# Query weights of two expert heads placed and used ahead of the gathers, and one third of a head norm done in tokens by heads

## The chip, the cores and the metric

The kernel runs on one core of one Trainium2 chip. The metric is the device time of one execution in microseconds (us). All times stated as moments (645.05, say) are counted from the start of the span of the one profiled execution.

## The reference

Two transformer blocks are computed one after the other on 256 tokens of width 1024, in fp32. What matters here is the end of the second block:

```python
mixed = jnp.concatenate([sb_o, hg_o, mem_o], axis=-1)   # sb_o: 8 heads of 64, each rms-normed over its 64
x = x + mixed @ w_out[l]
x = x + peer_ffn(rms_norm_2(x, norm_ffn_gain[l]), peer_w_query[l], peer_sub_keys[l], peer_u[l], peer_v[l])

# peer_ffn, for a block of 128 tokens: 8 heads, 128 + 128 keys, top 16, 16384 experts of width 1024
q = (x_blk @ w_query).reshape(b, t, PEER_HEADS, 2, HALF_KEY)
scores = jnp.einsum('bthcd,hcnd->bthcn', q, sub_keys)
top_s, top_i = lax.top_k(scores, 16)                     # in each half
best_s, pos = lax.top_k(cand_s, 16)                      # of the 16 x 16 sums of the two halves
expert_idx = jnp.take_along_axis(cand_i, pos, axis=-1)
gate = jax.nn.softmax(best_s, axis=-1)
act = gelu(jnp.einsum('btd,bthkd->bthk', x_blk, expert_u[expert_idx]))
out = jnp.einsum('bthk,bthkd->btd', gate * act, expert_v[expert_idx])
```

## The kernel before

The kernel is written engine by engine; each engine has its own stream of instructions, carried out in order, and semaphores tie them. Work is laid out by hand.

**Dense products.** Every weight tile (1 MB, 128 partitions by 2048) is split by ScalarE (`high_parts`, L1608) into a rounded high part `d_hi` in four quarters of 512 columns, and GpSimd (L2095, quarters 0 to 2) or VectorE (L2175, quarter 3) makes the low part `v_lo`. TensorE adds three products for each (L766). The cast of a quarter waits until TensorE has used the same quarter of the tile before (`s_dused`). The last such matrix is `out2`, in two halves of the columns, n = 0 and n = 1, each summing over eight k of 128 features. Its features are `hT_hi` and `hT_lo`: k = 0, 1 from memory attention, and then three groups of 512 numbers for each of 128 partitions (two k each): group 0 the HGRN heads, groups 1 and 2 the stick-breaking heads.

**The norm of a group** before `out2`. ScalarE squares the PSUM result (`square`, L1919); TensorE sums over the 64 features of each head with a block matrix and gets the sum for each feature and token, 128x512 (`head_sums`, L730); ScalarE takes the root of all 128x512 (`head_roots`, L1924); VectorE the reciprocal of all 128x512 (L2788) and multiplies (L2791, `mixed_normed`); ScalarE makes the high part (`mixed_high`, L1931), VectorE the low part (`mixed_low`, L2803). VectorE's order is: norm of group 0, norm of group 1, low part of 0, norm of group 2, low parts of 1 and 2. ScalarE's order is: high part 1, the four casts of the second half of `out2` n = 0, high part 2.

**The expert phase.** There are 16 units (8 heads by 2 blocks of 128 tokens) of 16 picks each, 256 picks in all. For each pick GpSimd issues one gather (`gather`, L2085) that fetches for every token the row of its expert, u and v together, 8 KB, into one of 15 row places (`row_slots`); VectorE takes the dot of u and the normed token (`expert_dots`, L2917); ScalarE applies gelu to four picks at a time (L2014) and puts the four weights on diagonals (L2022); TensorE adds diagonal times v into PSUM (`expert_values`, L1515). That frees the place, and the gather 15 picks later may be issued (`s_vused`). The places 9 and 10 are ring slots, 11 is the room of `d_hi`, 12 that of `v_lo` (`ada`), 13 is `memT` (free since the second memory projection), and 14 is `mix_rows`, the room of `hT_hi`, which `out2` reads to its end.

**The queries.** Each head needs 1 MB of query weights. SyncE loads them through two ring slots (L700): heads 0 and 1 as `out2` frees the slots, head h from 2 on when head h - 2 has been used (`s_wqu`). TensorE computes head 0 (`first_queries`, L1424) and head 1 (`queries`, L1450; `key_scores`, L730) before the picks begin, and head 2 in four parts between the picks of unit 0, head 3 in unit 2, and so on. ScalarE copies the result out (`queries_out`, L2001). VectorE finds the best keys (`best_keys`, L2848 to L2852), the best pairs and the expert numbers of unit u + 2 while it works on unit u.

ScalarE's order at the start of the expert phase is what the change touches most:

```python
row_to_bank(0)          # L2008
queries_out(1)          # L2001
gate_exp(0)             # L1993, softmax exponentials of units 0 and 1
gate_exp(1)
for u in range(UNITS):  # gelu, diagonals, ...
```

VectorE has `gates_of(0)` and `gates_of(1)` (L2899, L2900), which wait for these exponentials, directly before the first `expert_dots`. GpSimd waits once for the end of `out2`, then for the expert numbers of each unit, and issues the gathers in order.

Of the kernel before, what the change touches and what calls it, by code (L numbers as in the profile page):

```python
# [17 lines left out]
ALU = mybir.AluOpType  # L18
ACT = mybir.ActivationFunctionType
# [116 lines left out]
EARLY_TILE = [N_TILES + 1 + PEER_HEADS + j for j in range(len(EARLY))]  # L136
QUERY_SLOT = [(N_TILES + h % 2) % RING for h in range(PEER_HEADS)]


# [13 lines left out]
def psum_plan():  # L153
# [79 lines left out]
    for n in range(2):  # L233
        for tb in range(TB):
            group(("out2", n, tb), OUT2_BANK[n, tb])
    for name, bank in UNIT0_GROUPS:
        group(name, bank)
    for h in range(1, PEER_HEADS):
        group(("wq", h), 2 + h % 2)
        group(("keys", h), 2 + h % 2)  # L240
# [61 lines left out]
def build(nc, x_in, mem_in, pos_in, vec_in, ident_in, const_in, gain_in, w_in, uv_in, out):  # L302
    with ExitStack() as ctx:
# [31 lines left out]
        def take(*shape, at=None):  # L335
# [10 lines left out]
            if len(shape) == 3:  # L346
# [124 lines left out]
                      mix_rows.rearrange("p a n -> p (a n)")]  # L471

        def expert_rows(s):

            return row_slots[s % ROWS]
# [22 lines left out]
        halfms = stat[:, 164:166]  # L498
        sel = stat[:, 166:167]
        KINDS = {"cmp": 0, "slc": 16, "win": 32, "dsa": 0, "mem": 16}  # L500

# [62 lines left out]
        s_mprob = sem("mem_probs")  # L564
        s_sq = sem("mixed_squares")
        s_on = sem("mixed_normed")
        s_zln = sem("z_log")
# [5 lines left out]
        s_keys = sem("keys_loaded")  # L573
        s_wq = [sem(f"query_weights{i}_loaded") for i in range(2)]
        s_wqu = sem("query_weights_used")
        s_rows = sem("rows_gained")
# [85 lines left out]
        def _(sp):  # L662
# [31 lines left out]
            sp.dma_start(keep, w_in[KEYS_TILE]).then_inc(s_keys, 16)  # L694
            for h in range(PEER_HEADS):
                if h < 2:
                    sp.wait_ge(s_dused, 4 * (len(DENSE) - RING + h) + 4)
                else:
                    sp.wait_ge(s_wqu, h - 1)
                sp.dma_start(ring[:, QUERY_SLOT[h], :], w_in[QUERY_TILE[h]]).then_inc(s_wq[h % 2], 16)  # L700

# [8 lines left out]
        def _(pe):  # L710
# [58 lines left out]

            def project_rows(what, group, n, width=512):  # L770

                out_ = [begin((group, n, tb) if group in ("in", "out", "out2") else (group, tb))
                        for tb in range(TB)]
                for half in range(2):
                    d = DENSE_AT[(what, n, half)]
                    for r in range(4):
# [10 lines left out]
                        if k == KD - 1:  # L787
                            last = pe.drain()
                        last.then_inc(s_dused, 1)

            def project_features(what, n, groups):
# [569 lines left out]
            def head_sums(i):  # L1361
# [3 lines left out]
                end(mm(ps[:, :], con("pairblk"), sq[:, i, :]), ("ssq", i))  # L1365

            mem_values()
            stick_sums(0)
# [18 lines left out]
            stick_values(7)  # L1387
            head_sums(2)
            project_rows("out2", "out2", 0)
            acc = {(tb, c): banks[4 + 2 * tb + c] for tb in range(TB) for c in range(2)}  # L1390
# [49 lines left out]
            def queries(h, part):  # L1440

                name = ("wq", h)
                w = ring[:, QUERY_SLOT[h], :].rearrange("p (k n) -> p k n", k=KD)
                if part == 0:
                    begin(name)
                    pe.wait_ge(s_wq[h % 2], 16 * (h // 2 + 1))
                ps = banks[PLAN[name][0]]
                for k in (2 * part, 2 * part + 1):
                    for c in range(2):
                        last = nc.tensor.matmul(ps[:, c * T:(c + 1) * T], w[:, k, c * P:(c + 1) * P], hT[:, k, :],  # L1450
                                                start=(k == 0 and c == 0), stop=(k == KD - 1), skip_group_check=True)
                if part == 3:
                    end(last, name)
                    pe.drain().then_inc(s_wqu, 1)

            def key_scores(h):

                ps = begin(("keys", h))
                for tb in range(TB):
# [46 lines left out]
            for part in range(4):  # L1506
                queries(1, part)
            key_scores(1)

            def expert_values(s):  # L1510
# [10 lines left out]
            for u in range(UNITS):  # L1521
                if u % 2 == 1 and u // 2 + 2 < PEER_HEADS:
                    key_scores(u // 2 + 2)
                for s in range(u * TOPK, (u + 1) * TOPK):
                    if s % PART == 0 and u % 2 == 0 and u // 2 + 2 < PEER_HEADS:
                        queries(u // 2 + 2, s % TOPK // PART)
                    expert_values(s)
# [3 lines left out]
        def _(act):  # L1531
# [419 lines left out]
            nc.scalar.activation(stat[:, 152:153], one, ACT.Sqrt)  # L1951
            head_roots(2)
            mixed_high(1)
# [76 lines left out]
            row_to_bank(0)  # L2030
            queries_out(1)
            gate_exp(0)
            gate_exp(1)
            for u in range(UNITS):
                for part in range(TOPK // PART):
# [7 lines left out]
                    if g == PICKS // PART - 2:  # L2043
                        result(0, 0)
                        result(0, 1)
                if u % 2 == 0 and u // 2 + 2 < PEER_HEADS:
                    queries_out(u // 2 + 2)
# [4 lines left out]
        def _(pool):  # L2052
# [26 lines left out]
            def gather(s):  # L2079
# [3 lines left out]
                if s >= ROWS:  # L2083
                    pool.wait_ge(s_vused, s - ROWS + 1)
                nc.gpsimd.indirect_dma_start(  # L2085
                    expert_rows(s), None, uv_in,
# [16 lines left out]
        def _(dve):  # L2103
# [704 lines left out]
            mixed_normed(0, ("hgo",))  # L2808
            mixed_normed(1, ("sbo", 0))
            mixed_low(0)  # L2810
            mixed_normed(2, ("sbo", 1))
            mixed_low(1)
# [239 lines left out]
```

## Time and profile before

| | us |
|---|---|
| median of 3 runs | 1329.34 (1328.43 to 1330.27) |
| the profiled execution, its own time | 1326.55 |
| its span, first to last instruction | 1324.8 |
| TensorE busy | 1151.2 (87% of the span) |
| VectorE busy | 855.0 (65%) |
| GpSimd busy | 554.7 (42%) |
| ScalarE busy | 480.8 (36%) |
| mean granted TensorE clock | 0.937 of full speed |
| bytes moved by DMA | 381.17 MB, mean 288 GB/s |
| of the chain that ended last: TensorE 42%, DMA 36%, VectorE 13% | |

The span has two halves that look quite different: up to about 645 us dense products and attention, and from there the expert phase. Busy shares over the whole span mix the two, so the table alone doesn't tell what an edit in either is worth. The "idle" figure in brackets behind a row of the timeline is the time that the engine had no work just before it, with what ended the wait.

### The profile page before, as it was taken

To read this page: it belongs to the slowest core of one execution; us is meant where nothing else is said; L and a number is where in the kernel's file an instruction comes from. 1 tells how busy PE (TensorE), PEld (TensorE's weight loads), DVE (VectorE), ACT (ScalarE), POOL (GpSimd) and SP (SyncE) were. 2 spreads that over 40 slices of the span, in tenths; PEclk is the share of its full clock that TensorE was granted. 3 is DMA by queue.
4 is the path that set the end of the run, shared out by engine and by line. 5 is a ranking of instruction groups with operands and counts; after the bars stand their busy time and mean duration, and the time that the engine had idled before them with its cause. 6 is when DMAs were issued, how large, how long until landed. Compare 5 with 4: busy or idle time off the path is not lost.

```text
span 1324.8 us, 14114 instructions
## 1 busy us (share of the span) xinstructions
PE 1151.2 (87%) x4900; PEld 749.5 (57%) x4900; DVE 855.0 (65%) x1807; ACT 480.8 (36%) x1051; POOL 554.7 (42%) x479
## 2 busy tenths in 40 slices
PE   6889899899999989999788878888788878877877
PEld 3667777699978689876643333433334334333332
DVE  5777566545463388666776767767677776677553
ACT  3363133555544566655321222212222222222111
POOL 1457332476686555413433333333333433423330
PEclk8899787999999999999988999988989999979998
DMA  9533332645476443222599999999999999999993
GB/s 382 210 142 127 128 128 76 242 160 182 169 268 222 175 161 128 95 81 95 205 421 422 421 422 421 422 422 420 421 422 420 422 421 422 421 421 421 422 421 128
DMA packets 53463, 381.17 MB, mean 288 GB/s; under 512 B 6160, under 2 KB 6544, under 8 KB 7568
## 3 DMA queue, kind: packets, MB, share of 16 engines
q0 software_dynamic: 36864, 268.45, 48.7%
q1 hardware_dynamic: 15664, 111.00, 22.6%
q8 instruction: 39, 0.64, 0.2%
q10 hardware_dynamic: 864, 0.82, 0.2%
q14 instruction: 32, 0.26, 0.1%
HBM read 379.20 MB, written 1.05 MB: 287 GB/s over the span
## 4 chain that ended last, share of the span: by engine, by line
PE 42%; DMA 36%; DVE 13%; ACT 4%; issue 3%; POOL 1%; PEldq 1%; PEld 0%; SPq 0%; DVEq 0%; POOLq 0%; ACTq 0%
DMA arena<-uv_dram,arena 25%; PE bank L766 15%; PE bank L1515 8%; PE bank L730 7%; PE row_bank L766 6%; DMA mix_rows<-uv_dram,arena 6%; PE row_bank L730 2%; DMA ada<-uv_dram,arena 2%; DVE gain_rows_in L2917 2%; DMA ring<-uv_dram,arena 2%; DMA memT<-uv_dram,arena 2%; DVE arena L2313 1%; PE bank L853 1%; DVE arena L2788 1%; POOL v_lo L2095 1%
## 5 line engine op out<-in xcount | busy, mean ns | idle before, releaser
L1515 PE MATMUL bank<-arena 128*128 128x512 f32 x684 | 337.7, 645 | 86.9 <-ACT arena L2022 86.5
L2095 POOL TENSOR_TENSOR v_lo<-ring,d_hi 128x512 fp32r<-128x512 f32 x189 | 268.8, 1436 | 286.8 <-ACT d_hi L1608 218.7
L1515 PEld LDWEIGHTS bank<-arena 128*128 128x128 f32 x684 | 137.3, 206 | 270.7 <-issue 160.8
L2085 POOL DMA_INDIRECT arena<-uv_dram,arena x171 | 163.1, 954 | 290.6 <-PE bank L1515 265.7
L1608 ACT CAST d_hi<-ring 128x512 fp32r<-128x512 f32 x200 | 120.9, 620 | 137.0 <-PE bank L766 82.1
L2917 DVE SCALAR_TENSOR_TENSOR gain_rows_in<-arena,row_bank 128x1024 f32<-128x1024 f32 x86 | 104.9, 1220 | 81.2 <-DMA arena<-uv_dram,arena 81.1
L2014 ACT ACTIVATE arena<-arena 128x4 f32<-128x4 f32 x64 | 13.1, 205 | 388.0 <-DVE gain_rows_in L2917 388.0
L2175 DVE TENSOR_TENSOR v_lo<-ring,d_hi 128x512 fp32r<-128x512 f32 x63 | 59.5, 944 | 125.3 <-ACT d_hi L1608 118.2
L2917 DVE SCALAR_TENSOR_TENSOR arena<-arena,row_bank 128x1024 f32<-128x1024 f32 x85 | 103.6, 1219 | 48.9 <-DMA arena<-uv_dram,arena 48.2
L2022 ACT ACTIVATE arena<-ident,arena 128x128 f32<-128x128 f32 x256 | 81.7, 390 | 108.6 <-DVE arena L2924 108.6
L1515 PE MATMUL bank<-ring,arena 128*128 128x512 f32 x136 | 67.0, 634 | 11.5 <-ACT arena L2022 11.3
L730 PE MATMUL bank<-arena 128*128 128x128 f32 (+5 forms) x456 | 69.4, 302 | 3.4 <-issue 1.3
L730 PEld LDWEIGHTS bank<-arena 128*128 128x128 f32 (+1 forms) x456 | 58.2, 198 | 13.4 <-issue 8.6
L766 PE MATMUL bank<-hT_hi,d_hi 128*128 128x256 f32 x208 | 59.5, 286 | 2.1 <-DVE arena L2620 1.1
L766 PE MATMUL bank<-hT_lo,d_hi 128*128 128x256 f32 x208 | 58.8, 283 | 0.0
L766 PE MATMUL bank<-hT_hi,v_lo 128*128 128x256 f32 x208 | 58.8, 283 | 0.0
L766 PE MATMUL row_bank<-hT_hi,d_hi 128*128 128x256 f32 x192 | 54.9, 286 | 3.2 <-DVE hT_lo L2162 2.4
L766 PE MATMUL bank<-d_hi,hT_hi 128*128 128x512 f32 (+1 forms) x128 | 49.9, 390 | 5.2 <-POOL v_lo L2095 2.0
L766 PE MATMUL row_bank<-hT_lo,d_hi 128*128 128x256 f32 x192 | 54.3, 283 | 0.0
L766 PE MATMUL row_bank<-hT_hi,v_lo 128*128 128x256 f32 x192 | 54.3, 283 | 0.0
L1515 PEld LDWEIGHTS bank<-ring,arena 128*128 128x128 f32 x136 | 26.9, 201 | 47.2 <-issue 32.5
L1450 PE MATMUL bank<-hT,ring 128*128 128x256 f32 x224 | 52.4, 379 | 0.0
(404 smaller groups left out, 2304.4 us busy)
## 6 DMA issues: line engine op xcount, KB each, us to landing
ring<-w_dram SPq DMA_DIRECT2D x93, 1024.0 KB, 4.8
arena<-w_dram SPq DMA_DIRECT2D x9, 1024.0 KB, 10.5
arena<-uv_dram,arena POOLq DMA_INDIRECT x171, 24.2
x<-x_dram SPq DMA_DIRECT2D x1, 1024.0 KB, 6.0
arena<-mem_dram SPq DMA_DIRECT2D x1, 1024.0 KB, 16.6
out_dram<-x SPq DMA_DIRECT2D x2, 512.0 KB, 4.9
arena<-const_dram SPq DMA_DIRECT2D x1, 868.0 KB, 17.1
ring<-uv_dram,arena POOLq DMA_INDIRECT x34, 24.8
```

Of the source, the lines that this page charges most:

```text
L730: return nc.tensor.matmul(out_, lhsT, rhs, start=start, stop=stop)
L766: last = nc.tensor.matmul(out_, l, m, start=start and part == 0, stop=stop and part == 2, skip_group_check=True)
L853: last = nc.tensor.matmul(ps[g * HD:(g + 1) * HD, :], vcol("c", 4 * half + kk).to_broadcast([P, HD]), w[:, kk, :], start=(half == 0 and kk ...
L1450: last = nc.tensor.matmul(ps[:, c * T:(c + 1) * T], w[:, k, c * P:(c + 1) * P], hT[:, k, :], start=(k == 0 and c == 0), stop=(k == KD - 1) ...
L1515: last = nc.tensor.matmul(acc[tb, c][:, :], diag[:, s % N_DIAG, :], expert_rows(s)[:, D + c * 512:D + (c + 1) * 512], start=False, stop=(s ...
L1608: nc.scalar.copy(d_hi[:, r, :], dense_quarter(d, r)).then_inc(s_dhi, 1)
L2022: nc.scalar.activation(diag[:, s % N_DIAG, :], ident[:, :], ACT.Copy, scale=coefs[:, s:s + 1]).then_inc(s_diag, 1)
L2085: nc.gpsimd.indirect_dma_start(expert_rows(s), None, uv_in, bass.IndirectOffsetOnAxis(ap=ids[:, s:s + 1], axis=0)).then_inc(s_got[s % ROWS ...
L2095: nc.gpsimd.tensor_tensor(v_lo[:, r, :], dense_quarter(d, r), d_hi[:, r, :], ALU.subtract).then_inc(s_dpl, 1)
L2175: tt(v_lo[:, 3, :], dense_quarter(d, 3), d_hi[:, 3, :], ALU.subtract).then_inc(s_dvl, 1)
L2313: ins = stt(arow[:, n, :], w[:, kk, :], vcol("c", k), arow[:, n, :], ALU.mult, ALU.add)
L2917: stt(dotted[s % 2], expert_rows(s)[:, 0:D], 1.0, row_bank[:, :], ALU.mult, ALU.mult, accum_out=dots[:, s:s + 1]).then_inc(s_dot, 1)
```

## The change

Three things are done.

1. The 1 MB query weights of heads 2 and 3 no longer go through the ring but into row places 13 (`memT`) and 14 (`mix_rows`). Head 2's load is issued right behind the keys, head 3's once `out2` is complete. Heads 4 to 7 go through the ring, heads 4 and 5 released by the use of heads 0 and 1.
2. TensorE computes the queries of heads 2 and 3 directly after the key scores of head 1, ahead of the first expert values; none are computed in units 0 and 2 any more. Both use PSUM bank 2, so head 3 waits until ScalarE has copied head 2 out. ScalarE copies both out before `gate_exp(0)`. The gather into place 13 waits for the use of head 2's weights, that into place 14 for head 3's.
3. Group 2 of the head norm is done in tokens by heads: TensorE sums with the squares as the stationary operand and two columns of the block matrix as the moving one (four products, an 128x8 result); the root and the reciprocal are taken of 128x8; eight products (a column of the reciprocals spread over 64 columns, times the identity) bring them back to features by tokens in bank 0. They stand between k = 1 and k = 2 of `out2` n = 0. VectorE copies the values out of PSUM, then multiplies. The sums wait, as before, for the squares.

```diff
+EARLY_HEADS = {2: 13, 3: 14}
...
-            for h in range(PEER_HEADS):
-                if h < 2:
+            for h in (2, 0, 1, 3, 4, 5, 6, 7):
+                if h == 2:
+                    sp.wait_ge(w_used, N_WHOLE)
+                elif h < 2:
                     sp.wait_ge(s_dused, 4 * (len(DENSE) - RING + h) + 4)
+                elif h == 3:
+                    sp.wait_ge(s_dused, 4 * len(DENSE))
                 else:
-                    sp.wait_ge(s_wqu, h - 1)
-                sp.dma_start(ring[:, QUERY_SLOT[h], :], w_in[QUERY_TILE[h]]).then_inc(s_wq[h % 2], 16)
+                    sp.wait_ge(s_wqu, h - 3 if h < 6 else h - 1)
+                sp.dma_start(query_weights(h), w_in[QUERY_TILE[h]]).then_inc(
+                    s_wqe[h - 2] if h in EARLY_HEADS else s_wq[h % 2], 16)
...
+            def last_head_sums():
+                pe.wait_ge(s_sq, 3)
+                ps = begin(("ssq", 2))
+                for kk in range(2):
+                    for tb in range(TB):
+                        at = 2 * (2 * kk + tb)
+                        last = mm(ps[:, at:at + 2], sq[:, 2, kk * T + tb * P:kk * T + (tb + 1) * P],
+                                  con("pairblk")[:, 0:P:HD])
+                end(last, ("ssq", 2))
+            def last_head_rows():
+                pe.wait_ge(s_rec8, 1)
+                ps = begin(("roots",))
+                for kk in range(2):
+                    for tb in range(TB):
+                        for j in range(2):
+                            at = 2 * (2 * kk + tb) + j
+                            last = mm(ps[j * HD:(j + 1) * HD, kk * T + tb * P:kk * T + (tb + 1) * P],
+                                      root8[:, at:at + 1].to_broadcast([P, HD]), ident[:, :])
+                end(last, ("roots",))
...
-            head_sums(2)
-            project_rows("out2", "out2", 0)
+            last_head_sums()
+            project_rows("out2", "out2", 0, behind_pair=last_head_rows)
...
             key_scores(1)
+            for h in EARLY_HEADS:
+                for part in range(4):
+                    queries(h, part)
...
-                    if s % PART == 0 and u % 2 == 0 and u // 2 + 2 < PEER_HEADS:
+                    if s % PART == 0 and u % 2 == 0 and 4 <= u // 2 + 2 < PEER_HEADS:
                         queries(u // 2 + 2, s % TOPK // PART)
...
-            head_roots(2)
+            ps = wait_full(act, ("ssq", 2))
+            ins = nc.scalar.activation(root8, ps[:, 0:8], ACT.Sqrt, bias=eps, scale=1.0 / HD)
+            free(ins, ("ssq", 2))
+            wait_read(act, ("ssq", 2))
+            nc.scalar.copy(stat[:, 153:154], one).then_inc(s_root8, 1)
...
             queries_out(1)
+            queries_out(2)
+            wait_full(act, ("keys", 1))
+            queries_out(3)
             gate_exp(0)
...
+                elif s in EARLY_HEADS.values():
+                    pool.wait_ge(s_wqu, s - EARLY_HEADS[2] + 3)
...
             mixed_normed(1, ("sbo", 0))
+            dve.wait_ge(s_root8, 1)
+            nc.vector.reciprocal(root8, root8).then_inc(s_rec8, 1)
             mixed_low(0)
-            mixed_normed(2, ("sbo", 1))
+            ps = wait_full(dve, ("sbo", 1))
+            free(nc.vector.tensor_copy(root2[:, 2, :], ps[:, :]), ("sbo", 1))
+            wait_read(dve, ("sbo", 1))
+            ps = wait_full(dve, ("roots",))
+            free(tt(sq[:, 2, :], ps[:, :], root2[:, 2, :], ALU.mult), ("roots",))
+            wait_read(dve, ("roots",))
+            nc.vector.memset(coef[:, 0:1], 0.0).then_inc(s_on, 1)
             mixed_low(1)
```

## Rows read from the trace of the kernel before

**Rows 1.** The page, parts 2 and 3: DMA share by slice; the gather queue

```profile
DMA  9533332645476443222599999999999999999993
...
q0 software_dynamic: 36864, 268.45, 48.7%
```

**Rows 2.** Busy time by windows; columns: PE, PEld, DVE, ACT, POOL, PEclk, DMA share, GB/s

```profile
705.00:730.00 25.00, 17.26 (x37) 7.17 (x35) 19.65 (x54) 4.95 (x14) 8.35 (x9) 0.86 1.01 422
...
1280.00:1305.00 25.00, 20.46 (x43) 8.32 (x42) 12.98 (x24) 5.40 (x17) 2.02 (x3) 0.93 0.81 338
```

**Rows 3.** Waits of SyncE's DMA queue: total, times, longest us

```profile
SPq L700 <- PEq L1454: 300.7, 5, 83.7
...
SPq L700 <- PEq L1503: 24.6, 1, 24.6
```

**Rows 4.** DMA issues from 643 to 650: times, KB each, median us to landing

```profile
ring<-w_dram SPq DMA_DIRECT2D x1, 1024.0 KB, 5.0
```

**Rows 5.** Timeline of GpSimd: start us, us, what, [idle before, releaser]

```profile
645.05 1.49 POOL L2085 DMA_INDIRECT arena<-uv_dram,arena  x1 [19.08 <-DVE arena L2893]
...
664.27 0.93 POOL L2085 DMA_INDIRECT mix_rows<-uv_dram,arena  x1 [0.31 <-issue]
672.42 0.94 POOL L2085 DMA_INDIRECT arena<-uv_dram,arena  x1 [7.21 <-PE bank L1515]
675.80 0.94 POOL L2085 DMA_INDIRECT arena<-uv_dram,arena  x1 [2.45 <-PE bank L1515]
```

**Rows 6.** Timeline of TensorE, 640 to 672

```profile
646.99 7.07 PE L1450 MATMUL bank<-hT,ring 128*128 128x256 f32 x32
...
655.73 1.89 PE L1450 MATMUL bank<-hT,ring 128*128 128x256 f32 x8
668.36 4.64 PE L1515 MATMUL bank<-arena 128*128 128x512 f32 x5 [10.74 <-ACT arena L2022]
```

**Rows 7.** Timeline of ScalarE, 628 to 672

```profile
654.10 0.59 ACT L2001 COPY arena<-bank 128x512 f32<-128x512 f32 x1 [7.53 <-PE bank L1450]
654.70 1.28 ACT L1993 ACT_TABLE_LOAD   x1
```

**Rows 8.** Timeline of VectorE, 628 to 700

```profile
658.30 1.22 DVE L2917 SCALAR_TENSOR_TENSOR arena<-arena,row_bank 128x1024 f32<-128x1024 f32 x1
...
663.13 1.22 DVE L2917 SCALAR_TENSOR_TENSOR gain_rows_in<-arena,row_bank 128x1024 f32<-128x1024 f32 x1 [1.31 <-DMA arena<-uv_dram,arena]
...
667.71 0.16 DVE L2924 TENSOR_TENSOR arena<-arena 128x4 f32<-128x4 f32 x1
...
692.95 1.22 DVE L2917 SCALAR_TENSOR_TENSOR gain_rows_in<-arena,row_bank 128x1024 f32<-128x1024 f32 x1 [1.26 <-DMA arena<-uv_dram,arena]
...
695.78 1.22 DVE L2917 SCALAR_TENSOR_TENSOR arena<-arena,row_bank 128x1024 f32<-128x1024 f32 x1 [1.05 <-DMA arena<-uv_dram,arena]
```

**Rows 9.** Busy time by windows, columns as in rows 2

```profile
665.00:670.00 5.00, 1.64 (x2) 0.84 (x3) 4.76 (x16) 1.28 (x4) 0.21 (x1) 0.50 1.02 428
```

**Rows 10.** DMA issues from 644.8 to 646.5: the first gather alone

```profile
arena<-uv_dram,arena POOLq DMA_INDIRECT x1, 8.1
```

**Rows 11.** Timeline of all engines around the norm of group 2

```profile
605.02 1.12 PE L730 MATMUL bank<-arena 128*128 128x512 f32 x2 [0.69 <-ACT arena L1919]
...
608.20 3.35 DVE L2788 RECIPROCAL arena<-arena 128x512 f32<-128x512 f32 x1
...
611.64 0.62 ACT L1608 CAST d_hi<-ring 128x512 fp32r<-128x512 f32 x1 [0.73 <-PE bank L766]
...
612.43 0.91 ACT L1931 ACTIVATE hT_hi<-arena 128x256 fp32r<-128x256 f32 x2 [0.18 <-DVE stat L2796]
...
613.62 0.47 PE L766 MATMUL bank<-d_hi,hT_hi 128*128 128x512 f32 x1 [2.02 <-DVE hT_lo L2803]
```

**Rows 12.** Products with few columns, TensorE's timeline at 46 us

```profile
46.41 0.95 PE L730 MATMUL bank<-stat,arena 128*128 128x1 f32 x8
```

**Rows 13.** Groups by line and shape, 0 to 600: products of 64 by 128

```profile
L730 PE MATMUL bank<-ident,arena 128*64 128x128 f32 x48 | 4.4, 355 | 3.1 <-DVE arena L2456 3.1
```

More of the change, by code:

```diff
@@ L235, in psum_plan @@
             group(("out2", n, tb), OUT2_BANK[n, tb])
+        if n == 0:
+            group(("roots",), 0)
     for name, bank in UNIT0_GROUPS:
         group(name, bank)
-    for h in range(1, PEER_HEADS):
+    group(("wq", 1), 3)
+    group(("keys", 1), 3)
+    group(("wq", 2), 2)
+    group(("wq", 3), 2)
+    group(("keys", 2), 2)
+    group(("keys", 3), 3)
+    for h in range(4, PEER_HEADS):
         group(("wq", h), 2 + h % 2)
@@ L471, in build, with query_weights @@
                       mix_rows.rearrange("p a n -> p (a n)")]
+        def query_weights(h):
+            return row_slots[EARLY_HEADS[h]] if h in EARLY_HEADS else ring[:, QUERY_SLOT[h], :]
         def expert_rows(s):
@@ L499, in build @@
         sel = stat[:, 166:167]
+        root8 = stat[:, 168:176]
         KINDS = {"cmp": 0, "slc": 16, "win": 32, "dsa": 0, "mem": 16}
@@ L565, in build @@
         s_sq = sem("mixed_squares")
+        s_root8 = sem("last_head_roots")
+        s_rec8 = sem("last_head_reciprocals")
         s_on = sem("mixed_normed")
@@ L574, in build @@
         s_wq = [sem(f"query_weights{i}_loaded") for i in range(2)]
+        s_wqe = [sem(f"early_query_weights{i}_loaded") for i in range(2)]
         s_wqu = sem("query_weights_used")
@@ L768, in three_parts, with project_rows @@
                 return last
-            def project_rows(what, group, n, width=512):
+            def project_rows(what, group, n, width=512, behind_pair=None):
                 out_ = [begin((group, n, tb) if group in ("in", "out", "out2") else (group, tb))
@@ L789, in project_rows @@
                         last.then_inc(s_dused, 1)
+                        if k == 1 and behind_pair is not None:
+                            behind_pair()
             def project_features(what, n, groups):
@@ L1442, in queries @@
                 name = ("wq", h)
-                w = ring[:, QUERY_SLOT[h], :].rearrange("p (k n) -> p k n", k=KD)
+                w = query_weights(h).rearrange("p (k n) -> p k n", k=KD)
                 if part == 0:
                     begin(name)
-                    pe.wait_ge(s_wq[h % 2], 16 * (h // 2 + 1))
+                    if h in EARLY_HEADS:
+                        pe.wait_ge(s_wqe[h - 2], 16)
+                    else:
+                        pe.wait_ge(s_wq[h % 2], 16 * (h // 2 if h > 1 else 1))
                 ps = banks[PLAN[name][0]]
@@ L1456, in key_scores @@
             def key_scores(h):
+                wait_read(pe, ("wq", h))
                 ps = begin(("keys", h))
@@ L2045, in _ @@
                         result(0, 1)
-                if u % 2 == 0 and u // 2 + 2 < PEER_HEADS:
+                if u % 2 == 0 and 4 <= u // 2 + 2 < PEER_HEADS:
                     queries_out(u // 2 + 2)
```

## The prediction
> **What bounds the kernel now.** I began with the busy tenths of the page. The DMA line jumps to 9 at slice 20 and stays there to the end [rows 1]; that is where the gathers begin. The windows make it sharp: from 680 us on every window of 25 us has a DMA share of 1.01 at 420 to 423 GB/s, and only the window from 1280 falls off, when the last gathers drain [rows 2]. In the same window TensorE is busy 17.26 and VectorE 19.65 of 25 us. So the second half is bound by the DMA engines: 256 gathers carry 268.45 MB [rows 1], 1.049 MB each, which at 422 GB/s is 2.49 us. Whatever bytes leave this phase shorten it; whatever leaves the engines empty lengthens it.
>
> VectorE's timeline says the same from the other side: it waits for a landing again and again, at 663.13, 692.95, 695.78 [rows 8], and landings come 2.5 us apart.
>
> The waits of SyncE's queue show which other bytes share this phase. One load (head 2's) was released by the end of the first queries, and five (heads 3 to 7) by the end of `queries` [rows 3]. The first gather is issued at 645.05 [rows 5]; head 2's load falls in the same 7 us, landing after 5.0 us [rows 4]. So six loads of 1 MB compete with the gathers.
>
> The first half is bound by TensorE and by hand-overs between engines; the part that the change touches ends at 645, where the first expert numbers release the gathers.
>
> **The change part by part: the loads.** Heads 2 and 3 are loaded before 645. Head 2's goes out behind the keys, about 603; head 3's when `out2` is done, about 637, and 5.0 us [rows 4] end it at 642, before the gathers. Neither delays a load that someone waits for. SyncE's queue is in order, so I looked at what stands behind head 3's load: heads 4 and 5, released at the moments at which heads 2 and 3 were released before. In the gather phase four loads are left instead of six: 2 x 2.49 = **-4.98 us**. This rests on a saturated phase, which [rows 2] shows to the end.
>
> **The queries ahead of the picks, and the new wait.** TensorE is idle for 10.74 us before the first expert value at 668.36 [rows 6]. The queries of heads 2 and 3 go into that hole, but they are longer than it, and the cost lies on ScalarE: both copies now stand ahead of the gate exponentials. What is queued behind is everything: VectorE's gates wait for them, and its first dot stands behind the gates. By the rows: head 2 starts at 655.73, and a head takes 7.07 [rows 6], so 662.8; the copy takes 0.59 [rows 7] and frees the bank, 663.5 with the hand-over; head 3 to 670.6; copy, 671.3; table load 1.28 [rows 7], 672.6; two exponentials and the second gate, about 1.7 (estimate: VectorE's first dot was at 658.30, 2.3 us behind that table load's end [rows 7, 8], part of it other work). The first dot comes at 674.3 instead of 658.30, 16.0 later.
>
> What follows runs without waits for rows, as the first four have long landed: four dots of 1.22 are 4.9, then `best_keys`, which took from 664.3 to 667.71 [rows 8], 3.4; so the first weights are formed at 682.6 and not 667.71, 14.9 later. TensorE's first value follows 0.65 later [rows 6, 8], at 683.3. Its clock was at 0.50 after the idle time [rows 9], and it will again have been idle, 12 us, so I keep the pace of before: the place of row 0 was free 4.06 after the first value, that of row 1 3.38 after that [rows 5, 6]. The 16th gather (row 15) is then issued at 687.3, not 672.42, and row 16's at 690.7, not 675.80.
>
> Does the DMA run empty? Before, rows 15 and 16 landed at 692.95 and 695.78 [rows 8]; the queue held so much that both landings came 20 us behind their issue. Now what counts is how soon a gather into an empty queue lands. No row shows one. The nearest: the first gather, 8.1 us [rows 10], which shared the engines with head 2's load (2.5 us of it at most), and a load of the same bytes by SyncE, 5.0 [rows 4]. I take 8.1 - 2.5 = 5.6, and 5.8 with a little for sharing with the row before it. Row 15 lands at max(692.95, 687.3 + 5.8 = 693.1), row 16 at 690.7 + 5.8 = 696.5 against 695.78: **+0.7 us**. With 5.0 it is nil, with 8.1 it is 698.8, +3.0. From row 17 on the pace of the places (1.72 us a row at full clock, and no query part between) beats that of the DMA (2.49), so nothing is added.
>
> VectorE makes up what it lost: a group of four picks costs it 4 x 1.22 + 3.4 = 8.3 us at most, while the DMA takes 9.96 for four rows. In a window of 25 us it had 5.35 to spare [rows 2], so 16 us are regained in some 75 us, and before that the lead of 15 places covers it.
>
> The gathers into places 13 and 14 wait for heads 2 and 3: 663.2 and 671.0. The last of them was issued at 664.27 [rows 5]. GpSimd is in order, but behind it stands only row 15's gather, which is held until 687.3 anyway, and row 14's turn at the DMA comes at about 687. Cost nil; it would cost only if head 3 ended after about 683.
>
> **The norm of group 2.** Before, TensorE stands idle 2.02 us ahead of k = 4 at 613.62, released by VectorE's low part, which came behind the reciprocal of 128x512 at 608.20, 3.35 us [rows 11]. The new path takes the 3.35 away but puts work on TensorE in front of k = 2. The sums: four products are eight records, and eight records with one column took 0.95 [rows 12], against 0.57 to the next product for the old sums (605.02 to 605.59): +0.4. The rows: eight products, 16 records; records of 64 by 128 took 4.4 / 48 = 0.092 each [rows 13], those of [rows 12] 0.119: 1.5 to 1.9, I take 1.8, nearer to the second as the operands change with each. So k = 2 and 3 come 2.2 later, and k = 3 ends when k = 4 began before, 2.02 us after its old end, to 0.2. By then VectorE has the low part of group 1: the rows are there at 611.1, the product takes 0.7, and the low part 0.9, 612.9. What is late next is ScalarE's order: the casts of quarters 2 and 3 wait for k = 2 and k = 3 (the second was at 611.64 [rows 11], now 613.9), and high part 2 stands behind them, 614.6 instead of 612.43, 0.91 long; low part 2 then ends at 616.5, and k = 6 is due at 616.4. So it just fits. **+0.1 us**, from -1.0 (if the new products cost TensorE half as much, so that half of the idle time goes) to +1.5 (if the casts or the low part come late for k = 6).
>
> **The sum** is -4.98 + 0.7 + 0.1 = -4.2 us. The profiled execution took 1326.55 (span 1324.8), which is 2.8 under the median of 1329.34; the same difference on each gives 1322.4 for an execution like the profiled one and 1325.1 for the median. Bounds: -4.98 + 0 - 1.0 = -6.0 and -4.98 + 3.0 + 1.5 = -0.5, 1323.3 to 1328.8. A difference of 0.2% (2.7 us) is about what a measurement of this kernel can tell from none.
>
> **The rivals.** (A) *No gap at all.* If a gather into a nearly empty queue lands as fast as SyncE's load (5.0), or if the queue still holds a little at 691, the restart costs nothing: -4.9, 1324.4. For it: a landing is that of the slowest of 16 DMA engines, so that engine may still have work when the others are empty, and part of any gap is hidden. The Trainium skill's page "DMA: Bandwidth & Descriptors", section "Anatomy of one DMA", gives a fit of about 2.0 us plus the bytes over 436 GB/s for a GpSimd transfer, 4.4 us here by estimate; by it row 16 would be in time and this rival would hold. No row shows an unshared gather, and 8.1 speaks against it.
>
> (B) *The gap is long.* The first gather's 8.1 holds for every restart, and the ends of the norm's bounds come with it: -4.98 + 3.0 + 1.5 = -0.5, 1328.8, no difference that can be measured. For it: GpSimd's own description of the gather and the way to the engines is in the 8.1 and isn't shared.
>
> (C) *Slower: TensorE doesn't get its clock back.* Between row 15 and the point where the places have a lead again the DMA lives on TensorE's pace. At the clock of [rows 9] a row costs 3.38 us [rows 5], 0.89 more than the DMA needs. Before, it was back at 1.0 by 675. If it stayed low for n rows from 683, the DMA would lose 0.2 + 0.89 n; the gain is used up at n = 6, and it is slower by over 0.2% from n = 9. For n = 12: +10.9 - 4.9 = +6.0, 1335.3. Against it: nothing in the picks differs from before, where the clock rose in 4 us.
>
> (D) *The change of the loads does not count*, because the places and not the bytes set the pace. Then nothing is gained and the 16 us lateness is felt in part: about 1330, no measurable difference to slightly slower. Against it stands the share of 1.01 in all windows.
>
> **How the numbers follow.** Forecast 0.57, A 0.15, B 0.16, C 0.06, D 0.06. The forecast lies under 1326.7 (faster by over 0.2%) in four fifths of its cases: 0.47, and with A 0.62. The rest of it, B and half of D give 0.28 for within 0.2%; C and half of D, with some for what I don't see, 0.10 for slower. Predicted is 1325.1. Range 1322.8 to 1329.0: it takes in the bounds and B, and leaves out C, D and the far edge of A.
>
> **What would show it.** In the profile after: SyncE's waits for `queries` fall from five to three inside the phase, or the loads there from six to four; VectorE's first dot at about 674; row 15's gather at 687 and row 16's at 691, with a short dip of the DMA share in the window 685 to 695 and 1.01 behind it; the last landing about 4 us earlier than 1310; the first gather still at 645.2. The idle time of 2.02 before k = 4 is gone and 16 new records stand in its place. The prediction is wrong if the DMA share dips for over 3 us, if the first gather moves by over 1 us, or if the DMA rate changes.

## The result and the profile after

| | before | after |
|---|---|---|
| first comparison, 6 runs each, median us | 1328.51 (1326.45 to 1330.27) | 1320.70 (1317.95 to 1324.19) |
| ratio, 95% interval | | 0.9945 (0.9927 to 0.9963) |
| two further comparisons, ratio | | 0.9955 (0.9939 to 0.9970), 0.9960 (0.9945 to 0.9975) |
| all runs of this study | 119 runs, median 1326.7, mean 1326.9 | 27 runs, median 1321.5, mean 1321.1 |
| profiled execution, own time (span) | 1326.55 (1324.8) | 1321.45 (1319.7) |

The change gains 5.8 us, plus or minus 0.9 (95%, difference of the means over all runs), where 4.2 was predicted; the measured median lies below the range. A single execution scatters by 4 us to either side, so the two medians of the first comparison, 7.8 apart, say less than all runs together.

Now the profile after. At the start of the expert phase, first TensorE, then ScalarE, then VectorE, then GpSimd (start, us, what, idle before and its releaser):

```profile
655.88 7.07 PE L1500 MATMUL bank<-hT,memT 128*128 128x256 f32 x32
663.62 7.17 PE L1500 MATMUL bank<-hT,mix_rows 128*128 128x256 f32 x32 [0.68 <-ACT arena L2059]
682.90 17.80 PE L1569 MATMUL bank<-arena 128*128 128x512 f32 x36 [12.10 <-ACT arena L2080]
...
670.89 0.58 ACT L2059 COPY arena<-bank 128x512 f32<-128x512 f32 x1 [7.32 <-PE bank L1500]
```

```profile
673.31 0.16 DVE L2970 RECIPROCAL arena<-arena 128x1 f32<-128x1 f32 x1 [16.06 <-ACT arena L2051]
...
674.25 1.22 DVE L2988 SCALAR_TENSOR_TENSOR arena<-arena,row_bank 128x1024 f32<-128x1024 f32 x1
```

```profile
645.13 1.49 POOL L2148 DMA_INDIRECT arena<-uv_dram,arena  x1 [19.05 <-DVE arena L2964]
...
671.12 0.93 POOL L2148 DMA_INDIRECT mix_rows<-uv_dram,arena  x1 [6.92 <-PEq L1504]
686.95 0.93 POOL L2148 DMA_INDIRECT arena<-uv_dram,arena  x1 [14.90 <-PE bank L1569]
689.46 0.93 POOL L2148 DMA_INDIRECT arena<-uv_dram,arena  x1 [1.57 <-PE bank L1569]
```

SyncE's waits, to be set against [rows 3]: the end of `queries` now releases three loads and not five, so four loads are left in the phase, where there were six.

```profile
SPq L721 <- PEq L1504: 296.1, 3, 204.0
```

The timelines answer to [rows 5 to 8]. VectorE's 16.06 us of idle time behind ScalarE's exponentials is the new wait: it stands still until ScalarE has copied out head 3. Its first dot moves from 658.30 to 674.25, row 15's gather from 672.42 to 686.95. The windows show what the DMA engines make of it (columns as in [rows 2]):

```profile
680.00:685.00 5.00, 2.10 (x3) 1.07 (x4) 4.79 (x17) 1.28 (x4) 0.00 (x0) 0.50 1.01 421
685.00:690.00 5.00, 5.00 (x10) 2.11 (x10) 4.79 (x15) 0.20 (x1) 1.47 (x2) 0.79 0.95 349
690.00:695.00 5.00, 5.00 (x13) 2.13 (x12) 5.00 (x11) 1.46 (x5) 3.15 (x4) 1.00 0.99 401
```

They run short by 72 GB/s for 5 us and by 20 for the next 5, together 0.46 MB or 1.1 us of their time, and are full again from 695. The last landing releases VectorE's last dot at 1304.89, where it was 1309.98 before:

```profile
1309.98 1.22 DVE L2917 SCALAR_TENSOR_TENSOR gain_rows_in<-arena,row_bank 128x1024 f32<-128x1024 f32 x1 [2.33 <-DMA arena<-uv_dram,arena]
```

```profile
1304.89 1.22 DVE L2988 SCALAR_TENSOR_TENSOR gain_rows_in<-arena,row_bank 128x1024 f32<-128x1024 f32 x1 [2.33 <-DMA arena<-uv_dram,arena]
```

And the norm, TensorE's timeline, to be set against [rows 11]:

```profile
605.75 1.05 PE L752 MATMUL bank<-arena 128*128 128x2 f32 x8 [0.69 <-ACT arena L1973]
...
609.58 1.09 PE L752 MATMUL row_bank<-ident,stat 128*64 128x128 f32 x16
610.61 0.50 PE L788 MATMUL bank<-d_hi,hT_hi 128*128 128x512 f32 x1
```

The 16 records of the new rows hold up k = 2 by 1.03 us (609.58 to 610.61), and no idle time is left ahead of k = 4.

### The profile page after: what moved, and what is told of

Read it like the earlier page. It is cut to its first block, busy times and chain, and to the rows that moved or that the text cites. A ratio compares the mean times of both kernels' runs of the same rounds, so it can differ in the third digit from the quotient of the medians.

```text
span 1319.7 us, 14169 instructions
## 1 busy us (share of the span) xinstructions
PE 1146.9 (87%) x4922; PEld 750.1 (57%) x4922; DVE 848.9 (64%) x1808; ACT 480.6 (36%) x1052; POOL 556.9 (42%) x479
## 3 DMA queue, kind: packets, MB, share of 16 engines
HBM read 379.20 MB, written 1.05 MB: 288 GB/s over the span
## 4 chain that ended last, share of the span: by engine, by line
PE 49%; DMA 31%; DVE 11%; ACT 4%; issue 3%; POOL 1%; PEldq 1%; PEld 0%; SPq 0%; DVEq 0%; POOLq 0%; ACTq 0%
DMA arena<-uv_dram,arena 22%; PE bank L788 16%; PE bank L1569 11%; PE bank L752 7%; PE row_bank L788 7%; DMA mix_rows<-uv_dram,arena 4%; PE row_bank L752 2%; DMA ada<-uv_dram,arena 2%; DMA memT<-uv_dram,arena 2%; PE bank L1500 2%; DMA ring<-uv_dram,arena 2%; DVE gain_rows_in L2988 2%; DVE arena L2376 1%; PE bank L877 1%; PE bank L1255 1%
## 5 line engine op out<-in xcount | busy, mean ns | idle before, releaser
L1569 PE MATMUL bank<-arena 128*128 128x512 f32 x684 | 333.5, 639 | 83.1 <-ACT arena L2080 82.6
L2072 ACT ACTIVATE arena<-arena 128x4 f32<-128x4 f32 x64 | 13.1, 205 | 369.7 <-DVE gain_rows_in L2988 369.7
L1569 PE MATMUL bank<-ring,arena 128*128 128x512 f32 x136 | 63.6, 608 | 11.6 <-ACT arena L2080 11.6
L752 PE MATMUL bank<-arena 128*128 128x128 f32 (+6 forms) x462 | 69.3, 300 | 3.6 <-issue 1.4
L788 PE MATMUL bank<-d_hi,up_hi 128*128 128x512 f32 x128 | 51.2, 400 | 0.6 <-issue 0.5
```

Of the source, the lines that this page charges most:

```text
L752: return nc.tensor.matmul(out_, lhsT, rhs, start=start, stop=stop)
L788: last = nc.tensor.matmul(out_, l, m, start=start and part == 0, stop=stop and part == 2, skip_group_check=True)
L1569: last = nc.tensor.matmul(acc[tb, c][:, :], diag[:, s % N_DIAG, :], expert_rows(s)[:, D + c * 512:D + (c + 1) * 512], start=False, stop=(s ...
```

## The experiments

Every profiled execution was cut at three marks: the start of the sums of group 2 on TensorE (605.02 before), the first gather (645.05) and the start of VectorE's last dot, which waits for the last landing (1309.98). The first piece is the same code in all kernels. What is left behind the last dot is 14.4 to 15.0 us in fourteen of the seventeen profiles; it is 13.1 in the third of before, and 15.9 and 13.0 in the two with the hole filled. No part of the change goes with these three, and the table leaves this last piece out.

| kernel | start of the sums | sums to first gather | first gather to last dot | both, mean | difference to before by these | measured, mean of all runs |
|---|---|---|---|---|---|---|
| before, three profiles | 605.02, 607.19, 607.46 | 40.03, 41.66, 41.62 | 664.93, 664.17, 664.16 | 705.5 | | |
| after, three profiles | 605.75, 603.80, 606.30 | 39.38, 39.35, 39.37 | 659.76, 660.34, 659.49 | 699.2 | -6.3 | -5.8 ± 0.9 |
| loads only, two | 604.65, 608.80 | 41.61, 41.60 | 660.06, 660.58 | 701.9 | -3.6 | -2.7 ± 1.0 |
| norm only, two | 603.78, 603.01 | 39.40, 39.34 | 664.31, 664.08 | 703.6 | -1.9 | -1.0 ± 1.0 |
| hole filled, two | 601.72, 602.74 | 40.02, 40.00 | 664.27, 664.22 | 704.3 | -1.2 | -2.0 ± 1.4 |
| loads, hole filled | 604.79 | 40.03 | 660.06 | 700.1 | -5.4 | -6.5 ± 1.2 |
| two loads fewer | 601.36 | 41.66 | 660.87 | 702.5 | -3.0 | -2.7 ± 1.4 |
| gates ahead, two | 602.00, 604.28 | 39.37, 39.36 | 659.16, 659.62 | 698.8 | -6.7 | -7.3 ± 1.2 |
| waits added | 603.87 | 39.36 | 659.99 | 699.4 | -6.1 | -7.0 ± 1.7 |

The last column sets the mean of each kernel's runs (6 to 27) against the mean of 119 runs of before, with 95%. All rows agree with the sum of the two pieces within it.

**The kernel before, again.**

> The kernel before, unchanged, for a second profile and more times. If the profiled execution of before (1326.55) only happened to lie low, a second profiled one will lie near 1328.5, and its trace will show where the 2 us between executions sit: in the dense half (before the first gather), or in how far the last landing stands behind the mean of the 16 DMA engines. If the two halves are fixed and the profile was typical, the second lies within 0.5 us of the first.

Measured: median 1327.18 (12 runs), ratio to before 1.0004 (0.9991 to 1.0017); its profiled execution took 1329.59, span 1327.8. So 1326.55 was not low: over 119 runs the median is 1326.7. What was high was the median of three, 1329.34. The 3 us between the two profiles sit ahead of the first gather: 2.17 before the sums, 1.63 between the sums and the gather, and -0.76 behind it. The second of these is the interesting one. TensorE's timeline behind the idle 2.02 us, and its granted clock, in this execution and (last fence) in the first:

```profile
615.79 0.47 PE L766 MATMUL bank<-d_hi,hT_hi 128*128 128x512 f32 x1 [2.02 <-DVE hT_lo L2803]
...
617.18 0.63 PE L766 MATMUL bank<-d_hi,hT_lo 128*128 128x512 f32 x1
617.60 0.63 PE L766 MATMUL bank<-d_hi,hT_hi 128*128 128x512 f32 x1
```

```profile
617.00:620.00 3.00, 3.00 (x8) 2.32 (x8) 0.04 (x1) 0.62 (x1) 1.27 (x1) 0.50 0.28 115
```

```profile
617.00:620.00 3.00, 2.74 (x13) 1.99 (x12) 0.00 (x0) 1.48 (x3) 2.89 (x3) 1.00 0.00 0
```

About 1 us after the engine has resumed, the granted clock is at 0.50 (1.2 of 2.4 GHz), and some eight products start 0.43 us apart instead of 0.23. That is the 1.63. In the first profile the same idle time has no such effect. I had only the first when I predicted.

**The kernel after, again, twice.**

> The kernel after, unchanged. Theory 1 (the change is worth what the two traces show, 5.1 us, and the 7.8 between the medians holds some chance): over more runs the difference comes down to 5 to 6.5 us. Theory 2 (the traces miss something that most executions have): it stays at 7 to 8 us, and a second profile shows the last landing 6 us or more ahead of before's.

> The kernel after, for comparison on one chip. 660 us from the first gather to the last landing, 39.4 from the sums to the first gather, and 6 us less than before on the median (4.4 from the gather phase, 1.9 on average from the norm).

Measured: medians 1321.47 (9 runs) and 1321.94 (12 runs), ratios in the table above; 39.35 and 39.37 from the sums to the first gather, 660.34 and 659.49 from there. Theory 1 holds: over all runs the difference is 5.8, and part of the 7.8 was chance.

**Each part alone, twice.** The edits are the two halves of the diff: in one the norm of group 2 is that of before, in the other the loads, the order of the queries, and ScalarE's copies.

> The change without the norm: heads 2 and 3 loaded and used ahead of the gathers, the norm of group 2 as before. Theory 1: -4.98 for two loads, nothing for the gap since the slowest DMA engine still has work when the others run empty: -5 us. My prediction's sum: -4.98 + 0.7 = -4.3. Rival (the norm carries the surplus of the result): -4.3 or less here and -3 for the norm alone.

> loads_only once more. By the traces the loads are worth 4.4 us (664.3 to 659.9 from the first gather to the last landing), but the first measurement gave 2.6 plus or minus 0.8 on the mean. If the traces hold: -4.4. If something else is lost in most executions: -2.6 again.

Measured: medians 1324.14 and 1324.02 (12 runs each), ratios 0.9984 (0.9970 to 0.9999) and 0.9971 (0.9957 to 0.9984). From the first gather 660.06 and 660.58 us against a mean of 664.4 in before: 4.1 us, for which I had 4.3. But from the sums to the first gather both profiles have 41.6, the lower clock included.

> The kernel before with the norm of group 2 in tokens by heads and nothing else. From the two traces: from the start of the sums to k = 4 it took 8.60 us before and 7.6 after, so at most -1.0, and -0.6 if k = 6 then waits. My prediction's sum: +0.1. Rival (the norm carries the surplus): -3 us.

> norm_only once more. By the traces 39.4 us from the sums to the first gather against 41.6 in four of five profiles with the old norm and 40.0 in one: -1.9 on the mean. The first measurement gave -1.0 plus or minus 0.7.

Measured: medians 1326.09 and 1326.18, ratios 0.9991 (0.9978 to 1.0005) and 0.9992 (0.9978 to 1.0007). From the sums to the first gather 39.40 and 39.34. Against 40.03 it is 0.65, against 41.6 it is 2.3. The measured means of the parts (-2.7 and -1.0) add up to 2.1 less than the whole, and that is more than their errors together (1.6 to 1.7). The pieces of the traces do add up within 0.8 (-3.6 and -1.9 against -6.3). So the traces show that the parts add up, and the times speak against it by a little; what would make up the rest of the 2.1 stays open.

**The idle time filled.** Does the idle time ahead of k = 4 cost the clock? It can be filled without touching the norm:

```diff
                         last.then_inc(s_dused, 1)
+                        if k == 3 and what == "out2":
+                            for _ in range(2):
+                                mm(banks[0][:, :], con("pairblk"), con("hgmask")[:, 0:512])
```

> The kernel before, with two products of 128x512 that nobody reads put into TensorE's idle 2.02 us between k = 3 and k = 4 of out2. They take 1.7 us by the rows, so k = 4 is not delayed. Theory 3: the idle time costs more than itself, since in two of three profiles with the old norm TensorE's products take 0.63 instead of 0.39 us right behind it, and from the sums to the first gather it is 41.6 us there and 40.0 in the third. Then the filled hole gives 40.0 or a little more in every profile, no product of 0.63, and on the median -1 us against before. Rival (the slower products come by chance from anywhere, not from the hole): 41.6 is seen again or the median doesn't move.

> hole_filled once more, a second profile. Theory 3: 40.0 us from the sums to the first gather and no product of 0.63 us behind k = 4. Rival: 41.6, as in three of four profiles with the unfilled hole.

> loads_only with the idle time between k = 3 and k = 4 filled by two products of 128x512 that nobody reads. Theory 3: 40.0 us from the sums to the first gather, no product of 0.63 us, 660 from there to the last landing; on the mean 1.3 less than loads_only and 0.65 more than after. Rival (the slower clock comes by chance and the hole has nothing to do with it): 41.6 appears, and no gain on loads_only.

> The kernel before, a further profile. Theory 3 has no fixed result for it: 41.6 us from the sums to the first gather in three of four, 40.0 in one of four. From the first gather to the last landing 664.2 to 664.9.

Measured: hole filled 1324.17 (12 runs), ratio 0.9994 (0.9978 to 1.0009), which by itself can't be told from none, and 1321.83 in the one run of the second; loads with the hole filled 1320.59 (6 runs), ratio 0.9945 (0.9929 to 0.9961), where the loads alone had 0.9984 and 0.9971: 3.7 us less on the mean (plus or minus 1.5), for which I had 1.3. The sign is as expected; the size is more than the clock accounts for. TensorE's timeline of the first kernel, with the fill at 608.18:

```profile
608.18 1.88 PE L730 MATMUL row_bank<-arena 128*128 128x512 f32 x4
610.32 0.47 PE L766 MATMUL bank<-d_hi,hT_hi 128*128 128x512 f32 x1 [0.27 <-DVE hT_lo L2806]
```

All three profiles have 40.0 us from the sums to the first gather and no product of 0.63. With the idle time left in, five of six profiles (before twice, loads only twice, two loads fewer; not the first of before) have 41.6. In those five the granted clock falls to 0.50 between 0.0 and 1.1 us after k = 4 has begun; in none of the eleven profiles without the idle time does it fall there. Theory 3 holds: where the clock falls, 1.6 us of the norm's gain are the clock, and work that does nothing gets them as well. The further profile of before (before_3) had 41.62 and 664.16.

**The price of two loads.**

```diff
-            for h in range(PEER_HEADS):
+            for h in (0, 1, 4, 5, 6, 7):
...
-                    pe.wait_ge(s_wq[h % 2], 16 * (h // 2 + 1))
+                    pe.wait_ge(s_wq[h % 2], 16 * (h // 2 + 1 if h < 2 else max(h // 2, 1)))
```

> The kernel before without the loads of the query weights of heads 2 and 3; these heads are computed with the weights of heads 0 and 1, all else stays, queries in units 0 and 2. The price of the bytes alone: -4.98 us from the first gather to the last landing (664.2 to 664.9 before), so 659.5. If the gap at row 15 cost something in the change (660.06 in loads_only, 659.8 and 660.3 in after), this kernel is shorter than those by as much: 0.3 to 0.8. Rival (the places, not the bytes, set the pace): no change, 664.

Measured: 1323.78 (12 runs), ratio 0.9984 (0.9970 to 0.9999), and 660.87 from the first gather to the last dot, not 659.5: 3.5 us for two loads. My expectation was wrong in an instructive way. The first gather of before is issued at 645.05. The DMA queues of before from then to 648.1:

```profile
q1 hardware_dynamic: 116, 0.95, 86.1%
```

Only the queue of the loads moves bytes there, 0.95 MB of the 1.05 of head 2's load, and none of the gathers'. The load runs while the first gather's bytes aren't yet on their way; it is mostly free. Leaving out heads 2 and 3 takes away one load that cost some 1.0 us (3.5 - 2.49) and one that cost in full. In the change it is head 4's load that runs in this place, and those that are gone cost in full.

This kernel also has what no row of before showed, a first gather with no load beside it. It lands after 6.2 us, and not 8.1:

```profile
arena<-uv_dram,arena POOLq DMA_INDIRECT x1, 6.2
```

**The gates ahead of the copies.** Here only ScalarE's order differs from after:

```diff
-            queries_out(2)
-            wait_full(act, ("keys", 1))
-            queries_out(3)
             gate_exp(0)
             gate_exp(1)
+            queries_out(2)
...
                     on_diagonal(g)
+                    if g == 0:
+                        wait_full(act, ("keys", 1))
+                        queries_out(3)
```

> The kernel after, with ScalarE's gate exponentials ahead of the copies of heads 2 and 3, and the copy of head 3 behind the first diagonals. VectorE's first dot comes near 658 again, the first weights at 668, and TensorE's first value directly behind head 3's queries at 671 with its clock still high, row 15's gather at 673. The DMA engines don't run empty. If the gap of the change costs the mean of the engines 0.9 and the slowest nothing: 0 to -0.3 us against after. My prediction's term: -0.7. Rival (the gap costs in full): -1.5 or more.

> gates_ahead once more, on the same chip as the kernel after. From the traces: from the first gather to the last landing 659.2 in gates_ahead against 659.8, 660.3 and 660.0 in three executions with the change's order. So 0.9 us less than after_3 below, and about 7 less than before on the median. Rival (that 0.9 was chance): 660 again.

Measured: medians 1318.45 (8 runs) and 1319.39 (9 runs), ratios to before 0.9951 (0.9933 to 0.9969) and 0.9948 (0.9928 to 0.9968). TensorE's first expert value, the gathers of rows 15 and 16, and the windows in which after runs short:

```profile
667.16 14.16 PE L1569 MATMUL bank<-arena 128*128 128x512 f32 x32
```

```profile
669.41 0.94 POOL L2149 DMA_INDIRECT arena<-uv_dram,arena  x1 [1.10 <-PE bank L1569]
671.63 0.94 POOL L2149 DMA_INDIRECT arena<-uv_dram,arena  x1 [1.28 <-PE bank L1569]
```

```profile
685.00:690.00 5.00, 5.00 (x13) 2.24 (x12) 3.09 (x5) 1.28 (x1) 2.02 (x3) 1.00 1.02 423
690.00:695.00 5.00, 4.44 (x12) 1.70 (x11) 3.08 (x8) 2.32 (x6) 2.62 (x3) 1.00 1.01 421
```

The DMA share has no dip, and TensorE keeps its full clock up to 703 us. From the first gather it takes 659.16 and 659.62, on the mean 0.5 less than after (659.86), 5.0 less than before (664.4). So the gap costs 0.5 us at the end, though it takes 1.1 from the mean of the engines. Each landing is reported by 16 updates of a semaphore, which the trace keeps, and they show why: in after the last update of row 14 stands 1.40 us behind the mean of its sixteen, that of row 16 only 0.49, while in gates ahead it is 1.48 and 1.50. The slowest of the 16 still had work while the others stood empty. The two ranges (659.16 to 659.62, 659.49 to 660.34) overlap, but the landing of row 16, right behind the gap, says the same: 50.2, 51.1 and 50.6 us after the first gather in the three profiles of after, 50.2 and 50.0 with the gates ahead. Over all runs the mean is 1319.6 (17 runs) against 1321.1 (27), -1.5 ± 1.4. It is the fastest version here, but the times alone would not carry that: waits added, below, has the order of after and a mean of 1319.9.

**Is it TensorE's instruction fetch that holds the slowest DMA engine back?**

```diff
-                pe.wait_ge(s_diag, s + 1)
+                for _ in range(5):
+                    pe.wait_ge(s_diag, s + 1)
```

> The kernel after, with four more waits on a semaphore that is already there ahead of every expert value on TensorE, 1024 more entries in its instruction stream. Theory 4: the slowest DMA engine falls behind the mean by 1 us each time a piece of TensorE's instructions (16 KB, about every 60 us) is fetched, which makes 8 to 9 us at the last landing. With 1024 entries more there are four fetches more in the phase: the last landing is 4 us later, and 12 us behind the mean. Rival (the lag has another cause): no change, or the waits are merged by the build and nothing differs.

Measured: 1319.71 (6 runs), 659.99 from the first gather to the last dot, as in after. The queue of instruction fetches did carry more between 660 and 1290, first after, then this kernel:

```profile
q8 instruction: 10, 0.16, 0.1%
```

```profile
q8 instruction: 12, 0.20, 0.1%
```

Two more and not four, and no later landing. Theory 4 falls. Why one engine ends late stays open.

## Why the prediction was wrong, point by point

*The base.* The largest miss is no term of the change. I set 1329.34, a median of three, as the base and called the profiled execution's 1326.55 low by 2.8. Over 119 runs the median is 1326.7; the profiled one lay where most do. Of the 4.4 us between 1325.1 and 1320.7, 2.6 are this. The step "the same difference on each" failed: a spread of 1.8 us in three runs was no measure of how far three runs can lie from the rest. The range had no room for it: on 1326.7 the same sum gives 1322.5, and the range, moved down by 2.6, holds 1320.7. What is left of the 4.4 is the norm, below. The profiled execution lay at the median by chance; the second profile of before took 1329.59.

*Where the spread comes from.* The first piece, up to the sums, took 601.4 to 608.8 us in one and the same code, and the granted clock of one stretch goes with it. First a profile of before with 607.19 (before_again), then norm only with 603.78:

```profile
200.00:300.00 100.00, 92.97 (x578) 80.65 (x577) 58.21 (x90) 49.93 (x101) 47.87 (x33) 0.93 0.43 159
```

```profile
200.00:300.00 100.00, 91.32 (x610) 79.09 (x609) 62.66 (x97) 53.35 (x109) 49.57 (x35) 1.00 0.46 169
```

All six profiles with 0.93 there start the sums at 605.0 or later; of the eleven with 0.98 or 1.00 none does.

*The loads.* Right: -4.98 predicted, -5.0 in the version without a gap (659.4 against 664.4). That both vanished loads count in full is so because another load takes the place in front of the first gather's bytes; I had it from the moments of release and didn't see that the place was cheap (some 1.0 us and not 2.49).

*The new wait and its size.* Right: first dot 674.3 predicted and 674.25 measured, first value 683.3 and 682.90, row 15's gather 687.3 and 686.95, row 16's 690.7 and 689.46 (two rows at the low clock took 2.51 and not 3.38 between them, since the clock came back in between). How soon a gather into an empty queue lands was not the term that decided. Row 15's landed 5.7 to 6.0 us after its issue in the three profiles of after, where I had taken 5.8, but it stands 2.48 behind row 14's in each, the pace of a full queue, so its slowest engine had not been empty; row 16's took 5.9, 7.0 and 6.3. The cleanest measure is the unshared first gather of the kernel with two loads fewer, 6.2. The Trainium skill's fit on "DMA: Bandwidth & Descriptors" ("Anatomy of one DMA") would have 4.4 by estimate, and here the measurement decides. Rival A stood on that fit and on the slowest engine: the first half fell, the second was right, and the gap cost 0.5 of its 1.1. That my +0.7 is near this 0.5 is in part luck: it put row 16's landing at 696.5, and the landing came at 695.38.

*The gathers into places 13 and 14.* Right: issued at 663.27 and 671.12, at no cost.

*The norm.* Wrong: +0.1 predicted, -0.65 with the clock high and -2.3 with it low, about -1.9 on the mean of these profiles. Two steps failed. The new work on TensorE was priced too high. The rows' 16 records had 1.8 us, at 0.119 each, from products with one column; they took 1.03, or 0.064 each. I chose the dearer of two rows for want of a reason, and even the cheaper (0.092) was too dear. The new sums had +0.4 over the old ones, read to the start of the next product; but the old sums also held up the second product behind them. The twelfth, the last of k = 1, starts 3.47 us after the sums before (605.02) and 3.51 after (605.75), so they cost nothing:

```profile
608.49 0.39 PE L766 MATMUL bank<-d_hi,hT_lo 128*128 128x512 f32 x1
```

```profile
609.26 0.39 PE L788 MATMUL bank<-d_hi,hT_lo 128*128 128x512 f32 x1
```

So k = 4 begins 0.9 us earlier and not 0.2 later, and some 0.25 of it is lost again in k = 6 and k = 7, where I had put 0.1. The second step: the idle 2.02 us was priced at its own length. In five of the six profiles that have it, it cost TensorE its full clock right behind it, 1.6 us more. I had asked what the clock would do in the expert phase, where I changed a wait, and not in front of k = 4, where I took one away; the one profile that I had didn't show it.

*Rivals B, C and D.* None came true. The places got their lead back by 695, the clock was at 1.00 by 690, and the bytes, not the places, set the pace.

## What to carry to other kernels

In a phase whose DMA share is full, bytes moved out of it are worth their transfer time, and a late engine costs nothing until the queued transfers are used up: set the moment of the first reissue plus the time of a transfer into an empty queue against the moment at which the queue drains. Ahead of a phase bound by TensorE an idle stretch of some 2 us can cost nearly as much again by the clock behind it; two products that nobody reads are a cheap test of that. And when the gain looked for is a few us in 1300, take more runs than three as a base, and compare profiles piece by piece between marks, since neither three runs nor one profile's own time is a safe base.

## What the runs showed of the hardware

- TensorE's clock fell to 0.50 between 0.0 and 1.1 us after it had resumed work, behind an idle time of only 2.02 us (2.00 with the loads moved), in five of six executions, and not in the sixth.
- Eight fp32 products of a 128x64 stationary operand (one column spread over 64) with 128 columns took 1.03 us on TensorE, 0.13 for each.
- A load issued by SyncE just as the first gather is issued by GpSimd had moved 0.95 of its 1.05 MB before the gather's bytes began, 3.09 us after its issue. It cost some 1.0 us, where one amid the gathers cost 2.49.
- The gathers' last landing stands behind the rest: in after the DMA share falls from 1290 us on, and the last gather's landing releases the last dot at 1304.89. Of the 16 updates that report a landing, one comes late and ever later: at the last gather of before it stands 8.9 us behind the fifteenth. Its distance from the mean of the sixteen grows by some 0.9 us at the same gathers in all seventeen traces (the 157th, 181st, 201st and 225th to land among them), whatever stands around them. So it goes with the number of gathers; which mechanism is behind it wasn't found.
